# Attention's tail: last two strips interleaved by kind, first mixer tile prepared between the last units

## The reference

```python
x = x + _mixers(_rmsnorm(x, g_attn), w_in, g_out_a, g_out_b, sink_a, rpb_b, w_out)
h = _rmsnorm(x, g_ffn)
x = x + _expert_choice_ffn(h, w_router, w_gate, w_up, w_down)   # 16 experts
# in _mixers, from the projection of the normed rows:
oa = _window_attention(qa, ka, va, sink_a)          # 8 heads of 64, window of 128, a sink
ob = _neighbourhood_attention(qb, kb, vb, rpb_b)    # 8 heads of 64, on a grid 64 wide
merged = concatenate([_rmsnorm(oa, g_out_a), _rmsnorm(ob, g_out_b)])
return einsum('bse,ed->bsd', merged, w_out)
```

## Time and profile before

| | us |
|---|---|
| median of 3 runs | 2532.67 (2531.62 to 2532.73) |
| the profiled execution: time | 2533.57 |
| the profiled execution: span | 2531.8 |
| PE busy | 2451.8 (97%) |
| DVE busy | 1682.8 (66%) |
| ACT busy | 1471.7 (58%) |
| from the span's start to the first product of `mix` | 531.86 |

### The profile page before, as it was taken

One profiled execution on the slowest core, in us unless ns is written; L12 is line 12 of the kernel. 1 busy time (PEld: TensorE's weight loads), 2 busy tenths in 40 slices (PEclk: granted clock), 3 DMA queues, 4 the chain that ended last, 5 costly groups with the idle time before them and its releaser, 6 DMA issues.

```text
span 2531.8 us, 42849 instructions
## 1 busy us (share of the span) xinstructions
PE 2451.8 (97%) x16210; PEld 2195.4 (87%) x16210; DVE 1682.8 (66%) x2550; ACT 1471.7 (58%) x2081; POOL 161.3 (6%) x165
## 2 busy tenths in 40 slices
PE   8999999989949999999999999999999999999997
PEld 7888867667739999998999989899998989999896
DVE  6354279954677676676767667676666767666676
ACT  4333278877645556565555656556565655556574
POOL 0000000000010101010010101001010110101010
PEclk9999999999969999999999999999999999999998
DMA  5343254454456767676776767777676766767695
GB/s 187 108 142 108 75 170 162 143 196 135 134 196 232 252 232 251 224 256 228 256 246 232 255 223 252 234 253 248 232 249 230 252 234 246 254 233 245 230 324 212
DMA packets 99668, 542.37 MB, mean 214 GB/s; under 512 B 11072, under 2 KB 15552, under 8 KB 49408
## 3 DMA queue, kind: packets, MB, share of 16 engines
q1 hardware_dynamic: 92192, 515.30, 58.3%
q0 software_dynamic: 7392, 25.96, 4.7%
HBM read 500.32 MB, written 40.89 MB: 214 GB/s over the span
## 4 chain that ended last, share of the span: by engine, by line
PE 68%; DVE 2%; DMA 1%; ACT 0%; issue 0%; POOL 0%; DVEq 0%; SPq 0%; ACTq 0%; POOLq 0%
PE ex_gate_ps L1850 16%; PE ex_up_ps L1850 16%; PE ex_gate_ps L1852 7%; PE ex_up_ps L1852 7%; PE ex_down_ps L1864 2%; PE ex_down_ps L1867 2%; PE ex_down_ps L1865 2%; PE ex_down_ps L1866 2%; PE ex_down_ps L1868 2%; PE ex_up_ps L1864 2%; PE ex_up_ps L1867 2%; PE ex_up_ps L1866 2%; PE ex_up_ps L1868 2%; PE ex_up_ps L1865 2%; DVE fi_x L1815 0%; PE ex_turn_ps L1828 0%
## 5 line engine op out<-in xcount | busy, mean ns | idle before, releaser
L1706 DVE TENSOR_TENSOR ex_w_lo<-ex_w,ex_w_hi 128x2048 fp32r<-128x2048 f32 x384 | 880.0, 2292 | 448.0 <-ACT ex_w_hi L1623 446.6
L1623 ACT ACTIVATE ex_w_hi<-ex_w 128x2048 fp32r<-128x2048 f32 x384 | 733.5, 1910 | 208.7 <-PE ex_down_ps L1868 106.8
L1850 PE MATMUL ex_gate_ps<-ex_xt,ex_w_hi 128*128 128x384 f32 x2048 | 594.4, 360 | 1.5 <-DVE ex_xt L1712 1.5
L1850 PE MATMUL ex_up_ps<-ex_xt,ex_w_hi 128*128 128x384 f32 x2048 | 592.1, 359 | 0.0
L1852 PE MATMUL ex_gate_ps<-ex_xt,ex_w_lo 128*128 128x192 f32 x2048 | 513.8, 251 | 0.0
L1852 PE MATMUL ex_up_ps<-ex_xt,ex_w_lo 128*128 128x192 f32 x2048 | 512.7, 250 | 0.0
L1852 PEld LDWEIGHTS ex_gate_ps<-ex_xt,ex_w_lo 128*128 128x128 f32 x2048 | 392.6, 192 | 0.6
L1852 PEld LDWEIGHTS ex_up_ps<-ex_xt,ex_w_lo 128*128 128x128 f32 x2048 | 391.2, 191 | 0.0
L1850 PEld LDWEIGHTS ex_gate_ps<-ex_xt,ex_w_hi 128*128 128x128 f32 x2048 | 385.9, 188 | 2.3 <-issue 1.7
L1850 PEld LDWEIGHTS ex_up_ps<-ex_xt,ex_w_hi 128*128 128x128 f32 x2048 | 384.4, 188 | 0.0
L1641 ACT ACTIVATE ex_gate_low<-ex_gate_ps 128x384 f32<-128x384 f32 x128 | 62.9, 491 | 208.6 <-PE ex_gate_ps L1852 208.6
(11 more groups left out here) (318 smaller groups left out, 4041.8 us busy)
## 6 DMA issues: line engine op xcount, KB each, us to landing
ex_w<-in_w_experts SPq DMA_DIRECT2D x384, 1024.0 KB, 4.8
pj_w<-in_w_in SPq DMA_DIRECT2D x54, 512.0 KB, 3.6
at_bias<-in_near_bias SPq DMA_DIRECT2D x8, 1536.0 KB, 9.4
at_v_near<-v_scratch SPq DMA_DIRECT2D x24, 256.0 KB
o_scratch<-ld_out SPq DMA_DIRECT2D x24, 256.0 KB, 6.2
q_p<-in_x SPq DMA_DIRECT2D x12, 512.0 KB, 4.3
acc_scratch<-k_p SPq DMA_DIRECT2D x12, 512.0 KB, 5.1
h_scratch<-q_p SPq DMA_DIRECT2D x12, 512.0 KB, 2.9
```

The source lines that it names most:

```text
L1623: act.activation(w_hi[:, c % SLOTS, :], w[:, c % SLOTS, :], ACT.Copy).then_inc(hi_w, 1)
L1706: dve.tensor_tensor(w_lo[:, c % SLOTS, :], w[:, c % SLOTS, :], w_hi[:, c % SLOTS, :].bitcast(F32), ALU.subtract).then_inc(lo_w, 1)
L1850: nc.tensor.matmul(out[:, b, 0:2 * CAP], w_hi[:, slot, f], xt[:, k, :, :].rearrange("p h c -> p (h c)"), start=k == 0, stop=False)
```

## The change

The near blocks of strips 2 and 3 come in the order (2,0) (3,0) (2,1) (3,1) (2,2) (3,2) of (strip, kind) and are numbered so. The last block of kind 0 becomes block 17 and the last that reads the sample's q becomes block 21; blocks 22 and 23 are both of kind 2. Up to three tiles of values are loaded behind a block. ACT squares after steps 86 and 88 (N - 10, N - 8), makes the first weight split after step N - 2, table load and root after N - 1, the scaled copies after N + 1, and the second weight split last of all, after the copies of the turned tile. DVE makes the first low split after step N - 1 and the inverse root after step N. PE turns the tile in step N + 3, ahead of the last unit's turn. The functions `split` move above the steps, unchanged.

```diff
-    near = [Near(3 * strip + kind, kind, strip) for strip in range(STRIPS) for kind in range(3)]
+    places = [(strip, kind) for strip in (0, 1) for kind in range(3)]
+    places += [(strip, kind) for kind in range(3) for strip in (2, 3)]
+    near = [Near(n, kind, strip) for n, (strip, kind) in enumerate(places)]
...
+        SQUARE = [N - 10, N - 8]
...
-                for n in range(values, min(values + 2, V_SLOTS + done, len(V_TILES) * STRIPS)):
+                for n in range(values, min(values + 3, V_SLOTS + done, len(V_TILES) * STRIPS)):
...
-                if u == N - 1 or u == N:
-                    k = u - (N - 1)
-                    if k == 0:
-                        act.wait_ge(lead.o_in[0], 16)
+                if u in SQUARE:
+                    k = SQUARE.index(u)
+                    act.wait_ge(lead.o_in[0], 16)
                     act.activation(lead.merged[:, k * HALF:(k + 1) * HALF], lead.o[0][:, k * HALF:(k + 1) * HALF],
                                    ACT.Square, accum_out=lead.ss[:, k:k + 1]).then_inc(lead.squared, 1)
-                if u == N + 2:
+                if u == N - 2:
+                    split(0)
+                if u == N - 1:
                     act.wait_ge(lead.squared, 2)
                     act.activation(lead.rt[:], lead.ss[:], ACT.Sqrt, bias=shared.eps[:],
                                    scale=1.0 / HALF).then_inc(lead.root, 1)
-            split(0)
-            act.wait_ge(lead.refined, REFINE)
-            for k in range(2):
-                c = slice(k * HALF, (k + 1) * HALF)
-                act.activation(lead.merged[:, c], lead.o[0][:, c], ACT.Copy,
-                               scale=lead.rs[:, k:k + 1]).then_inc(lead.normed, 1)
-            split(1)
+                if u == N + 1:
+                    act.wait_ge(lead.refined, REFINE)
+                    for k in range(2):
+                        c = slice(k * HALF, (k + 1) * HALF)
+                        act.activation(lead.merged[:, c], lead.o[0][:, c], ACT.Copy,
+                                       scale=lead.rs[:, k:k + 1]).then_inc(lead.normed, 1)
+
             for k in range(2):
                 act.wait_ge(lead.turned, k + 1)
                 act.activation(lead.m_hi[:, 4 * k:4 * k + 4, :].rearrange("p j c -> p (j c)"), lead_ps[k][:],
                                ACT.Copy).then_inc(lead.hi_m, 1)
+            split(1)
...
-                if u == N + 3:
+                if u == N - 1:
+                    split(0)
+                if u == N:
                     dve.wait_ge(lead.root, 1)
                     inverse_root(dve, lead.refined, 0, lead.ss[:], lead.rt[:], [lead.tmp[:, i, :] for i in range(3)],
                                  lead.rs[:], 1.0 / HALF)
-            split(0)
...
+                if u == N + 3:
+                    pe.wait_ge(added, 2 * N)
+                    for k in range(2):
+                        pe.wait_ge(lead.normed, k + 1)
+                        for j in range(4):
+                            c0 = (4 * k + j) * P
+                            last = nc.tensor.transpose(lead_ps[k][:, j * P:(j + 1) * P], lead.merged[:, c0:c0 + P], ident[:])
+                        last.then_inc(lead.turned, 1)
                 if u >= OUT:
...
-            pe.wait_ge(added, 2 * N)
-            for k in range(2):
-                pe.wait_ge(lead.normed, k + 1)
-                for j in range(4):
-                    c0 = (4 * k + j) * P
-                    last = nc.tensor.transpose(lead_ps[k][:, j * P:(j + 1) * P], lead.merged[:, c0:c0 + P], ident[:])
-                last.then_inc(lead.turned, 1)
```

More of the change, by code:

```diff
@@ L737, in _, with split @@
         def _(act):
+            def split(j):
+                act.wait_ge(lead.w_in[j], 16)
+                act.activation(lead.w_hi[j], lead.w[:, j, :], ACT.Copy,
+                               scale=shared.gain_out[:, j:j + 1]).then_inc(lead.hi_w, 1)
             for u in range(STEPS):
@@ L796, in _, with split @@
             dve.wait_ge(negated, 2)
+            def split(j):
+                dve.wait_ge(lead.hi_w, j + 1)
+                dve.scalar_tensor_tensor(out=lead.w_lo[j], in0=lead.w[:, j, :], scalar=shared.gain_out[:, j:j + 1],
+                                         in1=lead.w_hi[j].bitcast(F32), op0=ALU.mult,
+                                         op1=ALU.subtract).then_inc(lead.lo_w, 1)
             for u in range(STEPS):
```

## The result

The changed kernel took **2539.68 us** (median of 10 runs, 2537.66 to 2545.46), the kernel before 2532.57 (10 runs, 2530.75 to 2535.89): a ratio of 1.0025, interval 1.0017 to 1.0033. That is 7.1 us **slower**, and the forecast was 2531.7, in a range that ended at 2533.6.

A forecast was written before the change was run, and what follows sets the result against it. PE was taken to bound the kernel, with a hole between attention and mixers. Mixers 1.69 earlier, less 0.2 for squares, left 1.5; the clock rises kept 1.0, so 2532.67 became 2531.7, range 2529.8 to 2533.6.

The forecast's parts named there:

- Step (e): Strip order and third value load in attention: covered by SP's idle time, they cost nothing.
- no DMA waits in blocks 14 to 20: Sign of a right forecast, in attention: nothing there waits for loads.
- (a): W_out and first split on ACT: lands 5.3 after issue, at S+5.93; ACT waits 0.33, split done at S+7.08.
- S: Moment SP issues the store of block 21, from which the tail is counted; forecast at 511.45.
- (b): ACT's step 95, then table load and root of 1.60, no further drain counted: root done at S+10.38.
- (c): Step 96 to mixers: o copy link 1.24, last scaling S+15.77, first product S+18.72, 1.69 earlier than before.
- (d) Squares: Two ACT squares of 0.63 moved to steps 86 and 88: they cost 0.2, leaving a gain of 1.5.
- (f) The clock: Clock rises in mixers and experts: of 1.5 gained, 0.47 to 1.5 is kept; 1.0 taken.
- Rival 3: PE starves under W_out's loads in steps 92 to 96, an "issue" stall of 1.9: 2533.6, chance 0.18.
- Rival 4: Table switch drains ACT another 1.28 ahead of two flips PE needs; 0.2 left, 2532.5, chance 0.05.
- Rival 1: Nothing kept: W_out lands after 6.1, squares cost 0.5, both clock rises stand still; 0.1 gained, 2532.5, chance 0.15.
- the chance of 0.03 for slower: Whole kernel slower by more than 5.1 us, from two cases together or a clock fall elsewhere.

The follow-up runs named there:

- e1: The kernel before with the new order of strips and three value loads behind a block, its tail unchanged; 2539.02 us, ratio 1.0022.
- e3: The changed kernel with value slots counted free by what has been read, so strip 3's loads start earlier; three loads behind a block; 2532.93 us, ratio 1.0003.
- e4: As e3, the changed kernel with earlier value loads, but two loads behind a block instead of three; 2533.04 us, ratio 1.0002.
- e8: The changed kernel with each value tile loaded by four DMAs of one grid row, order and slots unchanged; 2532.24 us, ratio 0.9994.
- e5: The kernel before with the new order and e3's earlier value loads, two behind a block, none of the preparation moved; 2533.82 us, ratio 1.0006.
- e6: e4 with the first weight split, on ACT and DVE, put back behind all steps; 2531.99 us, ratio 0.9998.
- e7: e5 with squares at steps 86 and 88, table load and root at N + 1, DVE's second low split before its low parts; 2531.02 us, ratio 0.9994.
- e9: e7 with the value tiles loaded by grid row, as in e8; 2530.32 us, ratio 0.9986.

## Why the prediction was wrong

**Step (e), order and values: the step that failed.** It said "strip 3 is needed from block 17 on and loaded behind blocks 13 and 14" and "Cost nothing". Both places were right; the conclusion lacked a term. The load was priced by SP's issue (0.8 us each; in after it was 1.2 to 1.3) and its landing by nothing. Block 17's first mixing comes 22.4 us after the first issue (473.8 against 451.4), a lead of four blocks where it was eight. The six tiles took 26.9 from the first issue to the release of PE (451.4 to 478.3), so PE stood 4.6 and then worked slowly: 6.64 of the 7.1. Bytes over the rate would not have warned, for they make 19.9, less than the lead. But the trace of the kernel before had the same six tiles at some 30.4 from the first issue to the last bytes, so the term could have been read there. The prediction named "no DMA waits in blocks 14 to 20" as a sign of being right and did not work it out. Runs e1, e3, e4 and e8 show this cause: with it 6.6, without it, in two different ways, nothing.

**Steps (a) to (c), the tail: right in order, wrong in sum.** 1.69 was forecast for the start of the mixers, 0.2 came.

- (a) W_out took 6.2 to land and ACT stood 1.21 for it: the end of the range named there (6.1 and 1.13), not the 5.3 that was taken. Against S the split starts at 6.82 and not at 5.93, 0.9 late. That the two loads of o were no longer under way did not shorten it.
- (b) The root ends at S+10.99 (532.29) against 10.38; table load and root are 1.6 as read. Of the 0.9, 0.3 was caught up in step 95.
- (c) The link from one o copy to the next was taken as 1.24 and is 2.05 (532.46 to 534.51). The reason is a price that the forecast did not have: the split made PE stand 2.24, table load and root 1.91, and the clock fell between the two. Eight mixing products still take 0.66 behind the first pause (530.04); the granted clock is 1.00 until 530.6 and 0.50 from there, and behind the second pause they take 1.12. The turns start 1.50 behind the first scaled copy, where the earlier trace rows have 0.85 (526.72 - 525.87), as the last mixing now stands in front of them. The last scaling ends at S+17.49 (538.79) for 15.77, the first product starts at 20.34 for 18.72.
- A gain was missed as well. The order alone gives 1.05 (e1, e5), which the forecast never priced by itself; so the moved preparation did not gain little, it **lost** 0.85. Split and table load left the end of the chain on ACT but entered the middle of it, ahead of flips for which PE waits. For the split, e6 shows that it pays to leave it behind them (M 1.16 shorter). For the table load it is argued: e7, which has it behind them, keeps the last mixing at 0.66 where e6 has 1.12, but turns and low parts stand differently there too.

**(d) Squares.** Forecast 0.2; in after PE never waits for ACT between 495 and the last units' 2.24, so it is not held by the squares of steps 86 and 88, and e7, which moves them too, came out within 0.2 of its expected M. Right as far as that goes; no run moved the squares alone.

**(f) The clock.** A third of the saving (0.5 of 1.5) was taken to be lost at the two rises. In after, the rise in the mixers comes at 547.7, 6.0 behind the restart (before: 3.1), and that of the experts 3.9 behind theirs (before: 5.5). So the rises move with the work, and neither distance is fixed. These rows of after answer to the earlier trace rows:

```profile
541.60:547.60 6.00, 5.96 (x14) 4.78 (x15) 3.50 (x9) 5.10 (x9) 1.22 (x3) 0.50 0.91 293
547.60:550.00 2.40, 2.40 (x11) 1.94 (x11) 2.35 (x2) 2.40 (x4) 0.00 (x0) 0.98 0.70 259
```

By 7/16 of the difference that is an estimated 1.3 us lost at the first rise and 0.7 won at the second; over 11 runs e7 and e9 kept 2.0 of 2.5 and 2.55 of 2.6. e5 and e6 scatter around that (-0.8 of 1.0, 1.0 of 1.4), so the share of two thirds (1.0 of 1.5) that (f) applied is neither borne out nor excluded.

**The rivals.** Rival 3 had the sign, with the wrong place and mechanism: no wait of PE with reason "issue" is among those of steps 92 to 96. Rival 4: the table load takes 1.28 and the root starts 0.02 after it, in after, and 0.01 in e7; the further drain of 1.38 that the Trainium skill names (ScalarE: Activation LUTs, What ACT_TABLE_LOAD costs) shows in neither. Rival 1's tail, nothing kept, is what came. None of the four looked at the strips' values, and so none could give 7 us; the chance of 0.03 for slower was too small for a change that moves six loads' deadline by four blocks. It also had no room: the forecast and the four rivals already sum to 1.00.

## What to carry to other kernels

When an order of work is changed, write down for each load its issue, the time to landing **that this very load shows in the trace, among its neighbours**, and its first use. The issue instruction's cost is no stand-in for the landing, and bytes over the rate alone can fall short (19.9 for 26.9 us here). A low DMA share while loads were in flight was the sign here that they ran on few engines; splitting them along a dimension that spreads made the same queue fast enough. Preparation for the next stage was cheap here where it stood behind what the bound engine still waited for; moved ahead of it, it took the clock down too.

## What the runs showed of the hardware

- In the wait of 4.6 us the granted clock fell from 1.00 to 0.50 at 476.0, when PE had stood for 2.2 us; it was back at 482.8, 4.4 us after the restart. In the tail of after PE stood 2.24 us, worked on at full clock for 1.0 and fell to 0.50 at 530.6; in e6 it fell at about 520.0, 0.6 us behind a single pause of 1.73. After the restart in the mixers half clock lasted another 6.0 us.
- Six tiles of 256 KB, each one DMA, moved at 102 GB/s when nearly alone, and slower while a bias load of 1536 KB ran: 26.9 us in all, 7 more than that rate gives for them and for what stood ahead of them. The bias load issued behind them needed 15.7 us in after and 8.8 in e8, where the tiles were split; the one issued just ahead of them needed 8.3 and 10.0.
- In several traces PE stands once or twice early in attention with reason "issue": 1.86 in before and in e3, 1.58 and 1.41 in after, 1.32 and 0.83 in e1. Behind the pause of 1.58 in after the clock read 0.50 from about 353.1 to 356.5; behind that of 1.86 in before it stayed at 1.00. This stretch of after holds the pause of 1.41:

```profile
375.00:385.00 10.00, 8.60 (x122) 6.08 (x120) 7.70 (x33) 7.52 (x25) 0.00 (x0) 1.00 0.61 190
```

It costs 1.4 us there, nearly as much as the gain that was sought in the tail. The pauses (2.99 in after, 1.86 before), with the half clock behind the first, are part of why block 16's store of after stands 3.3 us behind that of before (475.38 against 472.04), ahead of any wait for values. That they are also what makes executions of one kernel differ isn't shown, as there is one trace of each; what decides where they fall stays open.
